# Attention by pairs of heads: packed scores and values, transposes on TensorE, division on GpSimd

## The reference

```python
s_lat = einsum('bqkgd,bskd->bkgqs', q_n, k_n) * ATT_SCALE      # head dim 64
s_lat = where(valid, s_lat, NEG_INF)
s_ctx = einsum('bqkgd,bckd->bkgqc', q_n, k_ctx) * ATT_SCALE
prob = softmax(concatenate([s_lat, s_ctx, sink], -1))[..., :-1]
return prob[..., :band] @ v_n + prob[..., band:] @ v_ctx
```

```python
for i in range(seq // 128):
    s = einsum('bhqd,bhkd->bhqk', q[:, lo:hi], k[:, :hi]) * scale   # + decay in fox
    p = softmax(where(mask, s, -inf))
    outs.append(einsum('bhqk,bkhd->bqhd', p, v[:, :hi]))
```

## Time and profile before

| | |
|---|---|
| median of 3 runs | 3331.6 us (3325.98 to 3335.49) |
| the profiled execution | 3316.05 us, span 3314.2 us |
| busy, share of the span | PE 82%, PEld 42%, DVE 31%, ACT 23%, POOL 7% |
| granted TensorE clock, mean | 0.916 of full |
| window attention | 879.55 to 989.41 us of the span |
| mla | 2890.16 to 2966.55 us |
| fox | 2988.37 to 3075.62 us |

### The profile page before, as it was taken

The page is one execution under the profiler, slowest core; times in us unless marked ns, Lnnn a source line. Parts: engine busy times, 40 slices in busy tenths (PEclk is TensorE's granted clock), DMA queues, the critical chain, the costliest instruction groups (busy, mean ns, idle before and its releaser), DMA issues. The chain is left out here.

```text
span 3314.2 us, 52634 instructions
## 1 busy us (share of the span) xinstructions
PE 2719.9 (82%) x19566; PEld 1380.7 (42%) x19566; DVE 1027.0 (31%) x2449; ACT 763.2 (23%) x1738; POOL 244.4 (7%) x245
## 2 busy tenths in 40 slices
PE   6777777765899993889888988998898599699999
PEld 2445454553684442323333322332333254467444
DVE  1264646462346425111111111111111512555012
ACT  2133333341240002222222212222222201433100
POOL 0030303040000000000000000000000101100000
PEclk8888888887899996999999999999999599787999
DMA  5100000001207314799999999499968421001112
GB/s 192 53 25 22 6 22 6 22 3 53 77 16 282 121 51 185 277 397 356 399 378 372 371 377 400 154 373 378 399 265 313 145 86 56 13 2 52 51 51 77
DMA packets 118956, 569.62 MB, mean 172 GB/s; under 512 B 13808, under 2 KB 17392, under 8 KB 67216
## 3 DMA queue, kind: packets, MB, share of 16 engines
q1 hardware_dynamic: 97184, 510.21, 39.3%
q10 hardware_dynamic: 15472, 36.16, 3.5%
q0 software_dynamic: 6144, 20.98, 1.7%
HBM read 760.50 MB, written 16.52 MB: 234 GB/s over the span
## 5 line engine op out<-in xcount | busy, mean ns | idle before, releaser
L1337 PE MATMUL moe_gu_ps<-expert_w,xgT 128*64 128x512 f32 x3008 | 682.3, 598 | 88.5 <-PEq L1302 88.5
L1337 PEld LDWEIGHTS moe_gu_ps<-expert_w,xgT 128*64 128x64 f32 x3008 | 246.1, 137 | 517.3 <-issue 517.2
L1363 PE MATMUL moe_down_ps<-expert_w,actT 128*64 128x512 f32 x1504 | 347.6, 599 | 68.1 <-PEq L1302 68.1
L1422 DVE TENSOR_TENSOR biased<-moe_gu_ps,b_gu 128x512 f32<-128x512 f32 x94 | 65.0, 692 | 932.7 <-DVEq L1302 932.7
L1363 PEld LDWEIGHTS moe_down_ps<-expert_w,actT 128*64 128x64 f32 x1504 | 114.4, 136 | 240.1 <-issue 240.1
L1384 ACT ACT_TABLE_LOAD x47 | 60.3, 1283 | 417.3 <-ACTq L1302 417.3
L1843 PE MATMUL ahead_ps<-hT,x 128*128 128x256 f32 (+1 forms) x288 | 128.0, 542 | 23.6 <-PEq L57 23.6
L1266 ACT ACTIVATE xgT<-moe_xg_ps,ffn_shift,ffn_gain 128x64 f32<-128x64 f32 x384 | 118.9, 424 | 42.0 <-PE moe_xg_ps L1260 42.0
L1388 ACT COPY actT<-moe_act_ps 128x256 f32<-128x256 f32 x94 | 35.0, 372 | 402.3 <-ACTq L1302 402.3
L386 PE MATMUL b2p_ps<-b_w,b_hT 128*128 128x512 f32 (+1 forms) x320 | 122.3, 545 | 1.8 <-PEq L57 1.8
L386 PE MATMUL gates_ps<-mix_w,hT 128*128 128x512 f32 x256 | 112.6, 596 | 0.7 <-PEq L57 0.7
(11 more groups left out here) (687 smaller groups left out, 3839.4 us busy)
## 6 DMA issues: line engine op xcount, KB each, us to landing
expert_w<-in_w_experts SPq DMA_DIRECT2D x576, 1024.0 KB
late_w<-in_w_late SPq DMA_DIRECT2D x12, 2048.0 KB, 8.2
b_gu<-in_b_experts ACTq DMA_DIRECT2D x96, 256.0 KB
b_w<-in_w_in SPq DMA_DIRECT2D x10, 2048.0 KB, 7.5
ada_w<-in_w_ada SPq DMA_DIRECT2D x6, 2048.0 KB, 12.6
slot_rows<-yb ACTq DMA_DIRECT2D x94, 128.0 KB, 6.2
mix_w<-in_w_in_tok SPq DMA_DIRECT2D x5, 2048.0 KB, 10.1
x<-in_w_rkv SPq DMA_DIRECT2D x5, 1536.0 KB, 7.2
```

The costliest lines, as they stand in the source:

```text
L1337: last = nc.tensor.matmul(ps_gu[SLOTS * j:SLOTS * j + SLOTS, half, :], xgT[:, k, :], w[:, i, at:at + 512], start=(k == 0), stop=(k == KD - 1),
L1363: last = nc.tensor.matmul(ps_dn[SLOTS * j:SLOTS * j + SLOTS, :], actT[:, half, q, SLOTS * a:SLOTS * a + SLOTS], w[:, i, at:at + 512], star ...
L1422: step(nc.vector.tensor_tensor(biased[:, :], ps_gu[:, half, :], b_gu[:, half, :], ALU.add))
```

## The change

`attention_stage` takes pairs of heads. In the window stage a pair is one query head of each key head, and `qT` loses its zeroed copy: each head's scores use 64 rows, head 0 the upper and head 1 the lower half of the array, written into separate banks. In mla and fox a pair is two neighbouring heads, whose scores still use 96 or 66 rows. Values of both heads are issued in turn into the two column halves of `ps_o`, and copied out as 128 rows at once. VectorE no longer makes `diag`. It makes only the inverse of the sums, for both heads at once; GpSimd multiplies the probabilities by it in place, and TensorE transposes them against the constant identity. `masked`, `prob` and `probT` hold as many pairs as they held heads; `ps_s` holds one pair in the window stage and two in mla and fox. To match, `host_layout` orders the sinks and the rows of `w_up_att` by pair.

The diff, cut to its core (the removed lines of `attention_stage` stand above):

```diff
+def attention_stage(nc, name, pairs, scale, ident, width, early=None):
...
+    deep = 1 if width > 512 else 2
+    room = 1024 if width > 512 else 512
...
+        masked = held.enter_context(nc.sbuf_tensor(f"{name}_masked", [P, 2, 2, width], F32))
+        prob = held.enter_context(nc.sbuf_tensor(f"{name}_prob", [P, 3, 2, width], F32))
+        probT = held.enter_context(nc.sbuf_tensor(f"{name}_probT", [P, 2, 2, width], F32))
+        col = held.enter_context(nc.sbuf_tensor(f"{name}_col", [P, 3, 6, 2], F32))
+        ps_s = held.enter_context(nc.psum_tensor(f"{name}_s", [P, deep, 2, room], F32))
...
+                def turn(p, j):
+                    pe.wait_ge(s["shared"], 2 * p + j + 1)
+                    if 2 * p + j:
+                        pe.wait_ge(s["probT"], 2 * p + j)
+                    for t in range(len(pairs[p]["v"][j])):
+                        last = nc.tensor.transpose(ps_t[:, t * P:(t + 1) * P], prob[:, p % 3, j, t * P:(t + 1) * P], ident)
+                    last.then_inc(s["turned"], 1)
+                for p in range(n + 3):
+                    if p < n:
+                        if p >= deep:
+                            pe.wait_ge(s["maxed"], 2 * (p - deep) + 2)
+                        at = 0
+                        for keys in zip(*pairs[p]["keys"]):
+                            w, done = keys[0].shape[1], 0
                             while done < w:
                                 part = min(w - done, 512 - at % 512)
...
+                                for j in range(2):
+                                    last = nc.tensor.matmul(ps_s[:, p % deep, j, at:at + part], pairs[p]["q"][j],
+                                                            keys[j][:, done:done + part], start=(at % 512 == 0),
+                                                            stop=True, skip_group_check=True)
...
+                    if 2 <= p <= n + 1:
+                        turn(p - 2, 0)
+                    if p >= 3:
+                        r = p - 3
+                        pe.wait_ge(s["probT"], 2 * r + 2)
+                        if r >= 2:
+                            pe.wait_ge(s["done"], r - 1)
+                        blocks = len(pairs[r]["v"][0])
+                        for t in range(blocks):
+                            for j in range(2):
+                                last = nc.tensor.matmul(ps_o[HD * j:HD * j + HD, r % 2, 0:P], pairs[r]["v"][j][t],
+                                                        probT[:, r % 2, j, t * P:(t + 1) * P], start=(t == 0),
+                                                        stop=(t == blocks - 1), skip_group_check=True)
                         last.then_inc(s["values"], 1)
+                    if 2 <= p <= n + 1:
+                        turn(p - 2, 1)
 
...
+                        it, w = pairs[p], wide(p)
+                        if p >= 3:
+                            dve.wait_ge(s["shared"], 2 * (p - 3) + 2)
+                        for j in range(2):
+                            dve.wait_ge(s["scores"], p + 1)
...
+                        if it["sinks"] is not None:
+                            dve.wait_ge(s["negated"], 2 * p + 2)
+                            nc.vector.tensor_tensor(both(p, SINK), it["sinks"], both(p, NEGMAX), ALU.add) \
+                                .then_inc(s["sink_in"], 1)
+                    if 1 <= p <= n:
+                        q = p - 1
+                        dve.wait_ge(s["probs"], 2 * q + 2)
+                        whole = SUM
+                        if pairs[q]["sinks"] is not None:
+                            whole = DEN
+                            dve.wait_ge(s["sunk"], q + 1)
+                            nc.vector.tensor_tensor(both(q, DEN), both(q, SUM), both(q, SINK), ALU.add).then_inc(s["den"], 1)
+                            dve.wait_ge(s["den"], q + 1)
+                        nc.vector.reciprocal(both(q, INV), both(q, whole)).then_inc(s["inverse"], 1)
+                    if p >= 3:
+                        r = p - 3
+                        dve.wait_ge(s["values"], r + 1)
+                        if pairs[r]["gate"] is None:
+                            nc.vector.tensor_copy(pairs[r]["out"], ps_o[:, r % 2, 0:P]).then_inc(s["done"], 1)
...
+            @block.gpsimd
+            def _(pool):
+                for p in range(n):
+                    pool.wait_ge(s["inverse"], p + 1)
+                    for j in range(2):
+                        nc.gpsimd.tensor_scalar(prob[:, p % 3, j, 0:wide(p)], prob[:, p % 3, j, 0:wide(p)], c(p, INV, j),
+                                                None, ALU.mult).then_inc(s["shared"], 1)
...
+                def keep(p, j):
+                    act.wait_ge(s["turned"], 2 * p + j + 1)
+                    if p >= 2:
+                        act.wait_ge(s["values"], p - 1)
+                    nc.scalar.copy(probT[:, p % 2, j, 0:wide(p)], ps_t[:, 0:wide(p)]).then_inc(s["probT"], 1)
...
+                def raise_e(p, j):
+                    act.wait_ge(s["negated"], 2 * p + j + 1)
+                    if p >= 3:
+                        act.wait_ge(s["turned"], 2 * (p - 3) + j + 1)
+                    nc.scalar.activation(prob[:, p % 3, j, 0:wide(p)], masked[:, p % 2, j, 0:wide(p)], ACT.Exp,
+                                         bias=c(p, NEGMAX, j), accum_out=c(p, SUM, j)).then_inc(s["probs"], 1)
...
+                for p in range(n + 2):
+                    for j in range(2):
+                        if p >= 2:
+                            keep(p - 2, j)
+                        if p < n:
+                            raise_e(p, j)
+                    if p < n and pairs[p]["sinks"] is not None:
+                        act.wait_ge(s["sink_in"], p + 1)
+                        nc.scalar.activation(both(p, SINK), both(p, SINK), ACT.Exp).then_inc(s["sunk"], 1)
...
-        qT = sb("q_turned", [P, 2, 4, SEQ])
...
+            lo, hi = max(0, b - 1), min(NT_X, b + 2)
+            mask = {0: masks[:, 640:1152], NT_X - 1: masks[:, 0:512]}.get(b, masks[:, 0:640])
+            rows = [slice(HD * kv, HD * kv + HD) for kv in range(2)]
+            for h in range(4):
+                pairs.append(dict(
+                    q=[qT[r, h, b * P:(b + 1) * P] for r in rows], keys=[[kcT[r, :], keyT[r, lo * P:hi * P]] for r in rows],
+                    v=[[kvc[:, t, P + HD * kv:P + HD * kv + HD] for t in range(NT_C)] +
+                       [qkv[:, t, 640 + HD * kv:640 + HD * kv + HD] for t in range(lo, hi)] for kv in range(2)],
+                    mask=mask, sinks=sinks[:, 2 * h:2 * h + 2], out=attT[:, h, b * P:(b + 1) * P], gate=None))
+        attention_stage(nc, "window", pairs, HD ** -0.5, ident, 640, early=early)
...
-            @block.gpsimd
-            def _(pool):
-                for kv in range(2):
-                    rows = slice(HD * (1 - kv), HD * (1 - kv) + HD)
-                    nc.gpsimd.memset(qT[rows, kv], 0.0).then_inc(s["zero"], 1)
-                    pool.wait_ge(s["zero"], kv + 1)
...
-                        for kv in range(2):
-                            rows = slice(HD * kv, HD * kv + HD)
-                            nc.scalar.copy(qT[rows, kv, :, m * P:(m + 1) * P],
-                                           ps[rows, m % 2, 0:512].rearrange("p (j t) -> p j t", j=4))
+                        nc.scalar.copy(qT[:, :, m * P:(m + 1) * P], ps[:, m % 2, 0:512].rearrange("p (j t) -> p j t", j=4))
...
-def heads_at(t, b, h):
-    return t[HD * (h % 2):HD * (h % 2) + HD, h // 2, b * P:(b + 1) * P]
```

More of the change, by code:

```diff
@@ L417, in attention_stage @@
         MAX, NEGMAX, SUM, SINK, DEN, INV = range(6)
-        with stage(nc, name, "scores", "maxed", "negated", "probs", "turned", "probT", "values", "done", "den",
-                   "diag") as (s, block):
+        with stage(nc, name, "scores", "maxed", "negated", "sink_in", "sunk", "probs", "den", "inverse", "shared", "turned",
+                   "probT", "values", "done") as (s, block):
             if early is not None:
@@ L423, in _, with wide, c, both @@
                     early(sp)
-            def c(i, what):
-                return col[:, i % 3, what:what + 1]
-            def rows(i):
-                return slice(HD * items[i]["half"], HD * items[i]["half"] + HD)
+            def wide(p):
+                return P * len(pairs[p]["v"][0])
+            def c(p, what, j):
+                return col[:, p % 3, what, j:j + 1]
+            def both(p, what):
+                return col[:, p % 3, what, :]
             @block.tensor
             def _(pe):
-                for i in range(n + 3):
-                    if i < n:
-                        if i >= 2:
-                            pe.wait_ge(s["maxed"], i - 1)
-                        it, at = items[i], 0
-                        for keys in it["keys"]:
-                            w = keys.shape[1]
-                            done = 0
+                def turn(p, j):
[12 more added lines that the diff above has]
```

(14 more changed lines are left out.)

123 lines of the change are left out of this document (30 added, 93 removed).

## The result

The changed kernel takes 3250.03 us in the median of 4 runs (3244.63 to 3254.58), the kernel before in runs beside it 3328.79 (3325.15 to 3335.49): ratio 0.9761, 95% interval 0.9737 to 0.9784. That is 79 us less; 98 were forecast. The profiled execution took 3250.61 us.

The account below looks back on a forecast made before the run. TensorE's queue was taken to bound the three attention stages. Savings of 47.3 (window), 21.7 and 28.8 (block-causal) and 0.5 us (rope) sum to 98.3, from 3331.6 to 3233 us; range 3208 to 3275.

Parts of the forecast that it names:

- TensorE's queue bounds the stages before; half the turning and half the values go: Three attention stages: TensorE 97 to 98% busy; turning and values each fall from 4n to 2n units a pair.
- Row halves overlap: 2n units: Window scores: two heads' halves run together, 2n units a pair of n blocks; a unit is 0.11 us over 128 columns.
- Four changes of group a pair, 0.11 each: TensorE in all three stages: scores, turn, values, turn replace six groups, adding 0.44 us a pair at full clock.
- by columns the bounds are 0.86 and 2.02 us a head at n = 5; I take 0.86: GpSimd's multiplication of probabilities by the inverse, five-block window heads: price scaled from earlier operations at 1.03 and 2.42 us.
- the prediction's own chain: Window: scores, maxima, inverse, GpSimd twice, second turn across two periods; 6.6 us, 3.3 a pair at five blocks.
- So TensorE's shorter work still covers GpSimd: Attention stages: GpSimd's chain stays under TensorE's work, 3.3 against 3.74 us a five-block pair; one-block pairs about even.
- Filling and emptying of the window, 8 us: Window: first three rounds' waits and the end's extra work add 8 us to 54.6, giving 62.6.
- First block-causal stage 54.7, second 58.5: Stage lengths forecast: 42.2 us of pairs, 4.6 for filling, emptying and one-block waits, plus low clock; 21.7 and 28.8 less.
- low-clock term: Block-causal stages: extra time at the 1.2 GHz level in one- and two-block pairs, 7.9 us first, 11.7 second.
- Contention: Rival: GpSimd and VectorE slow each other, 25 us in the window, 5 in the others; time 3263, chance 0.20.
- row-halves rival: Window scores' row halves don't overlap, 2n units more a pair; time 3249, chance 0.08.
- Low clock in both block-causal stages: Rival: the 1.2 GHz level holds throughout both stages, 83.6 us each; time 3287, chance 0.07.

Follow-up runs that it names:

- e7: Changed kernel with turning again a matmul against the scaled identity made on VectorE, GpSimd dividing nothing; ratio 0.9831 to the kernel before, window 85.5 us.
- e4: Changed kernel with window scores on all 128 rows again, zero-padded, two heads one after the other; ratio 0.9787 to the kernel before, window 83.5 us.
- e1: Changed kernel with GpSimd multiplying only each head's first 128 columns, the rest left undivided; ratio 0.9748 to the kernel before, window 68.2 us.
- e6: Changed kernel with GpSimd multiplying by the constant 0.5 instead of the inverse; ratio 0.9767 to the kernel before, window 74.3 us.
- e11: e10 plus filler matmuls: 6 in each of the window's first three rounds, 2 per one- or two-block round; ratio 0.9702 to the kernel before.
- e10: Changed kernel with the previous pair's inverse between the two maxima and four-deep rings in the block-causal stages only; ratio 0.9749 to the kernel before.
- e5: Changed kernel with each pair's second head divided on VectorE, the first on GpSimd; ratio 0.9786 to the kernel before, window 81.0 us.
- e9: Changed kernel with each pair's first head divided on VectorE, the second on GpSimd; ratio 0.9736 to the kernel before, window 68.1 us.
- e12: e11 with each pair's first head divided on VectorE, between the maxima; ratio 0.9697 to the kernel before, window 75.1 us.
- e8: Changed kernel plus filler: 12 matmuls in each stage's first three rounds, 4 in later one- or two-block rounds; ratio 0.9775 to the kernel before.
- e3: Changed kernel with probabilities four pairs deep instead of three in all stages; ratio 0.9762 to the kernel before, window 73.8 us.

## Why the prediction was right, and where its numbers were not

*TensorE's queue bounds the stages before; half the turning and half the values go.* Right. The window has 144 turning instructions instead of 288, and e7 shows that what they return depends on the chain behind them.

*Row halves overlap: 2n units.* Right: 1.28 us against 2.17 (e4).

*Four changes of group a pair, 0.11 each.* 0.15 measured in e1: 0.2 us a pair.

**The step that failed: "by columns the bounds are 0.86 and 2.02 us a head at n = 5; I take 0.86".** It took 1.88, near the other end of the bounds. With it the prediction's own chain gives 4.9 + 2 x 1.88 = 8.7 (8.77 measured), 4.3 a pair, and not TensorE's 3.74. The reason given, that VectorE's operation here reads PSUM, speaks about contention, and the low value needed more than that none occurs: it needed a price for this operation. The two rows of before, at 1.03 and 2.42, are of an instruction with two scalar operations. The trace of before has it eight times, on the same shape (duration in ns, least, median and most):

```profile
L1690 POOL TENSOR_SCALAR f_k<-f_b,pair_cols,one_ka x6: 1032/1941/2632, 183.1 to 516.5; 128x768 f32<-128x768 f32 x6
```

The other two took 1.68 and 2.49 us. Only one of the eight is under 1.68, which is 1.40 at 640 columns, so the 1.03 that the low bound rests on was the exception. Why it was so short isn't explained by anything here. Even 1.40 puts the chain at 7.7 us, 3.85 a pair and over 3.74.

e1 prices the error: 9.0 us in the window, 2.5 and 2.0 in the other stages. That is too much for the window: e1's operation, at 0.60, is shorter than the 0.86 taken, and its window filled at 0.69 of the clock instead of 0.52. Against e6, which filled at the same clock, e1 is 6.1 us shorter. "So TensorE's shorter work still covers GpSimd" was wrong in all three.

*Filling and emptying of the window, 8 us.* Too small. The clock was taken as full after the first scores (0.98 over the stage before); it was 0.50 to 0.55 for 18 us. TensorE waited in these rounds (busy 9.84 of 14.30 us), and filler in the waits took the clock to 0.87 (e11 against e10, 0.52) and gave 2.5 us back, at its own cost. The window's miss is 14.8 us (77.4 for 62.6). Up to 9.0 are GpSimd's, with the clock that came earlier in e1. Some 2.8 are the rounds, 16 at 0.17 (3.91 for 3.74 at five blocks, 3.26 for 3.08 at four, both in e1). The other 3 are left in e1's filling and emptying, where the clock was still 0.69; how they divide isn't measured.

*First block-causal stage 54.7, second 58.5.* 53.8 and 63.6. Without its low-clock term the forecast is 46.8 for each, and e10's first stage, at 1.00 throughout, took 47.3. The near hit of the first stage is luck, two errors that cancel: GpSimd cost 2.5 us where nothing was put down, and the low level some 4.5 where 7.9 were (e1, at 0.87, took 51.3; the 4.5 is an estimate from these figures). In the second the size of the low-clock term failed too, the other way: "low through all two-block pairs" was 11.7 us, and the level also held through the first two 3-block rounds and returned while emptying, some 14.8 by the same estimate (61.6 in e1). GpSimd's 2.0 come on top. At a clock of 1.00 the stage takes 48.6 us (e11).

*Rivals.* Contention: VectorE's maximum stayed at 0.88, and GpSimd's 512 columns took 1.55 each also at the end of the window, where no maximum is left beside them (timeline, GpSimd):

```profile
958.08 4.64 POOL L522 TENSOR_SCALAR window_prob<-window_prob,window_col 128x512 f32<-128x512 f32 x3 [0.38 <-DVE window_col L507]
```

So it didn't happen in the changed kernel. It is real for another pair of instructions: with a VectorE division from SBUF to SBUF beside it (e5, e9, e12) GpSimd's took 0.36 us more, with the maximum from PSUM nothing. The Trainium skill (GPSIMD Engine Reference, opening table) puts the contention on VectorE instructions in a 2-port mode or with two SBUF inputs. The maximum, with one operand in PSUM, fits it; the division fits it if it ran in such a mode, which no run here shows. The price of that rival (3263), its range and the time of the row-halves rival (3249) were near the result for another reason. Low clock in both block-causal stages: it came true for a part of the second.

*The sum.* 98.3 forecast, 78.1 by the stages and 78.8 by the medians: window 32.4 for 47.3, 22.3 for 21.7, 23.3 for 28.8. Three quarters of the miss are the window's. The medians leave nothing that would have to be placed outside the stages; ScalarE's copies in the rope stage became one of 0.585 us, as said.

## What to carry to other kernels

When a step goes to an engine whose price no row shows, look at every execution of the nearest operation and not at two, and work the chain through with both bounds before choosing; if the bound flips the limit (here 0.86 gives TensorE, 2.02 GpSimd), the forecast is two cases and not one. With several engines in order there is more than one chain: list each ring that goes through the slow operation, with the queue order of the engines in it, since halving the work in one (e5) moves nothing while the other holds. And an edit that shortens TensorE's work makes gaps, which can cost the clock for longer than the gaps last; small useless matmuls in the waits gave 21 us in one stage here (e11 against e10). With more of them, in the changed kernel, the window and the first block-causal stage became 4 and 5 us longer at a higher clock (e8).

## What was not expected of the hardware

- GpSimd's one-operation TENSOR_SCALAR: 0.60, 0.92, 1.24, 1.56 and 1.88 us at 128 to 640 columns, with a column or a constant (1.81 at 640) as operand. VectorE's for 640 columns of the same data: 0.55.
- Rings of four without filler kept the granted clock at 1.00 in the first block-causal stage (e3 and e10: 46.7 and 47.3 us) and left it at 0.50 in most of the second (66.5 and 69.7), with the same order of work. The second has 66 rows in place of 96 and loads data in its first rounds (DMA share 0.17). Which of it, if either, decides stays open.
- TensorE looks busy at the low level (5.00 of 5.00 us from 2949 to 2954, at 0.50), since each pass is longer; only the granted clock tells that time is being lost.
